# A five-layer transformer kernel: where its two rotary layers make their tables and turn their tiles

## The chip, the cores and the metric

The kernel runs on one core of a Trainium2 chip. The metric is the device time of one execution in microseconds (us). The core has five engines: TensorE (PE), VectorE (DVE), ScalarE (ACT), GpSimd (POOL) and SyncE (SP), each with an instruction queue of its own. They are synchronized by semaphores that the kernel sets by hand.

## What is computed

Five layers over 512 tokens of width 1024, in float32: a first hybrid layer, and then layers 0 to 3 with four different mixers (mLSTM, sliding-window attention, HGRN2, differential attention), each with a feed-forward network (FFN) behind it. Two of them use rotary positions, layers 1 and 3. Cut to what matters here:

```python
def partial_rope(x, positions):           # first 16 of 64 channels of a head
    ang = positions[..., None] * inv      # inv: 8 frequencies
    cos, sin = jnp.cos(ang), jnp.sin(ang)
    x1, x2 = x[..., :8], x[..., 8:16]
    return concatenate([x1 * cos - x2 * sin, x2 * cos + x1 * sin, x[..., 16:]])

def swa_mixer(h, positions, w_in, sinks, w_out):      # layer 1
    proj = h @ w_in                                   # q: 1024, k: 128, v: 128 columns
    q, k = partial_rope(q), partial_rope(k)           # then attention in a window of 128, with sinks

def diff_mixer(h, positions, lam_init, w_in, lam_vec, norm_w, w_out):   # layer 3
    proj = h @ w_in                                   # q, k, v: 1024 columns each
    q, k = partial_rope(q), partial_rope(k)
    lam = exp(sum(lv[0] * lv[1])) - exp(sum(lv[2] * lv[3])) + lam_init
    a = softmax(q0 k0) - lam * softmax(q1 k1)         # causal, per head
```

## The kernel before

Activations lie transposed, 128 channels on the partitions by 512 tokens. Weights come in **slots** of 128 x 1024 (eight 128 x 128 chunks). SyncE loads a slot into `raw`, ScalarE rounds it into `w_hi` (L1202), GpSimd subtracts to get `w_lo` (`low`, L562), and TensorE takes three products per chunk (high by high, low by high, high by low, `slot_products`, L659 to L661). Four slots rotate (`RING`), so ScalarE's split of slot k + 4 waits until TensorE has used slot k. A tile of 128 output channels is one slot; it goes to one of four PSUM banks in turn, and the tile four later waits until VectorE has copied the bank out (`lin_free`).

A layer goes: input projection, mixer, output projection, layer norm, FFN up (44 slots), FFN down (8 tiles of 3 slots), layer norm. The next layer's input projection starts with three tiles (`EARLY`) that are multiplied chunk by chunk as the norm delivers them (L747 to L752). While the FFN runs, VectorE also computes the next layer's modulation from the `ada` weights (L2131) in `ada_raw` and `ada_acc`; TensorE sums it up behind the first down tile, and VectorE stores it in `mod` (L2137, L2170). Then `add_gated` copies the down tiles and keeps sums beside them (L1703 to L1739). ScalarE's part of that is `squares_beside`.

The order on every engine is the order of the code. There is no scheduler; whatever stands behind a waiting instruction on its engine waits too.

In the two rotary layers before the change:

- GpSimd fetches the positions (L625) at the start of the layer. VectorE makes the angles (`rope_tables`, L1936 to L1949: a conversion, ten operations with one source, six with two) right after its copy of tile 3 (`rope_between`), and ScalarE takes their sine and cosine (L1380) into `rope_cs`.
- VectorE's `keep` copies the tiles of the projection to `proj` (L1672). A tile is rotated by `turned_halves` on TensorE (L979: a product with a constant matrix that swaps the two halves, to bank 4 or 5) and three operations of `rope` on VectorE (L1957 to L1959).
- Layer 1 has 9 tiles (8 of queries, then the keys) and one value tile that is multiplied in four quarters (L716 to L718). TensorE turns two tiles behind each quarter, and the ninth at the end. Then VectorE copies the values (L1679), and the rotated keys to `swa_k` (L2204), and attention starts with a score product (L863).
- Layer 3 has 16 tiles (8 of queries, 8 of keys) and 8 value slots that give two groups of four value banks (L703 to L705, copied at L1685). Two tiles are turned behind each value slot. Then GpSimd makes each key tile's two padded copies (`df_k`, L631 and L634), VectorE and ScalarE compute lambda (`lambdas`), and attention starts (L863).

Of the kernel before, what the change touches and what calls it, by code (L numbers as in the profile page):

```python
# [8 lines left out]
F32 = mybir.dt.float32  # L9
# [7 lines left out]
P = 128  # L17
S = 512
# [35 lines left out]
SWA_TILES = [j * P for j in range(9)]  # L54
# [3 lines left out]
DIFF_TILES = [j * P for j in range(16)]  # L58
# [4 lines left out]
           2: (HGRN_TILES, HGRN_VALUES), 3: (DIFF_TILES, DIFF_VALUES)}  # L63
GATE_TILES = {0: [2048 + j * P for j in range(8)], 2: [3072 + j * P for j in range(8)]}
# [42 lines left out]
KEPT = {"ident": 128, "ones": 128, "block64": 128, "eps6": 1, "tiny": 1, "eps6_32": 1, "eps5": 1}  # L107
# [4 lines left out]
def constants():  # L112
# [35 lines left out]
    for at in (2, 4):  # L148
        layer[at, :, 0:128] = rope
        layer[at, :, 128:129] = inv  # L150
# [5 lines left out]
    return kept, big, layer  # L156
# [6 lines left out]
def mix_steps(part):  # L163

    return {"first": 2, 1: 1, 3: 1}.get(part, 0)
# [49 lines left out]
def program(nc, xT, wstream, ada, cols, kept, bigc, layerc, pos, yT, parts):  # L215
    slots_total = stream_length(parts)
    ctx = ExitStack()
    with ctx:
# [96 lines left out]

        ident, ones, block64 = kept_at("ident"), kept_at("ones"), kept_at("block64")
# [242 lines left out]
        def _(pool):  # L559
# [57 lines left out]
            for at, part in enumerate(parts):  # L617
# [18 lines left out]
                if part == 1:  # L636
                    low_to(first_slot + LEAD + 2)
                    nc.gpsimd.memset(swa_k[:, :, :, :], 0.0)
# [10 lines left out]
        def _(pe):  # L649
# [326 lines left out]
            def turned_halves(t):  # L976

                wait(pe, sm.rope_out, n["rope"] - 1)
                mm(bank[4 + n["rope"] % 2][:, :], lc[:, 0:128], proj[:, t, :], start=True,  # L979
                   stop=True).then_inc(sm.rope_mm, 1)  # L980
                n.add(rope=1)

# [141 lines left out]
            for at, part in enumerate(parts):  # L1124
# [14 lines left out]
                linear(len(tiles) - EARLY, h_hi, h_lo, [8])  # L1139
                if part == "first":  # L1140
                    first_values()
                elif part in (1, 3):
                    pe.wait_ge(sm.layer_const_loaded, 16 * n["lc"])
                    if part == 3:
                        pe.wait_ge(sm.lin_free, n["mt"])
# [1195 lines left out]
```

## Time and profile before

| | us |
|---|---|
| median of three runs (range) | 3570.35 (3568.2 to 3574.76) |
| the profiled execution | 3571.12 |
| its span on the core | 3569.1 |
| TensorE busy, share of the span | 3373.3, 95% |
| VectorE busy | 1700.5, 48% |
| ScalarE busy | 1218.1, 34% |
| GpSimd busy | 1314.2, 37% |
| mean granted clock of TensorE | 0.964 |

The page gives busy time per engine, the span in 40 slices and the costliest groups of instructions. The timeline lists instructions in order of time; in brackets stands how long the engine had been idle before one, and what released it. Matmuls are pipelined, and the duration of one in a row is longer than the distance to the next.

### The profile page before, as it was taken

How to read it: one execution, taken by the hardware profiler on the slowest of the kernel's cores; microseconds unless marked ns; L12 is line 12 of the kernel's file. 1: busy time of each engine (PE TensorE's matmuls, PEld its weight loads, DVE VectorE, ACT ScalarE, POOL GpSimd, SP SyncE). 2: the span in 40 equal slices, each digit the busy share in tenths (PEclk: the TensorE clock that was granted, in tenths of full speed). 3: DMA queues.
4: the chain of work that ended last, by engine and by line, in shares of the span. 5: the costliest groups of instructions: out<-in, count | busy, mean ns of one | idle time of the engine just before them, and what ended most of it. 6: DMA issues, size and time to landing. Idle time of an engine off the chain costs nothing.

```text
span 3569.1 us, 43233 instructions
## 1 busy us (share of the span) xinstructions
PE 3373.3 (95%) x15372; PEld 2673.9 (75%) x15372; DVE 1700.5 (48%) x2643; ACT 1218.1 (34%) x1906; POOL 1314.2 (37%) x603
## 2 busy tenths in 40 slices
PE   7987899999989999989999999999999998999998
PEld 6765578886757888767788878767888775668886
DVE  2344545512246554377655343556654347662223
ACT  3246433222234332336432243124332332643322
POOL 3430134443313444430444444433444443024442
PEclk9978999999999999989999999999999998999999
DMA  4310045532212554320455423102554331013332
GB/s 136 106 36 1 24 154 184 186 130 88 77 36 96 198 184 157 103 60 8 147 188 182 142 90 99 44 29 82 202 187 159 109 90 52 1 48 112 94 101 70
DMA packets 102534, 374.08 MB, mean 105 GB/s; under 512 B 11392, under 2 KB 11520, under 8 KB 102272
## 3 DMA queue, kind: packets, MB, share of 16 engines
q1 hardware_dynamic: 102240, 371.77, 31.8%
q8 instruction: 85, 1.39, 0.2%
q0 software_dynamic: 160, 0.52, 0.0%
q14 instruction: 49, 0.40, 0.0%
HBM read 370.15 MB, written 2.10 MB: 104 GB/s over the span
## 4 chain that ended last, share of the span: by engine, by line
issue 44%; PE 41%; POOL 13%; DVE 1%; ACT 1%; DMA 0%; POOLq 0%; SPq 0%; DVEq 0%; ACTq 0%
POOL w_lo L562 12%; PE bank L659 11%; PE bank L661 11%; PE bank L660 11%; PE bank L1092 1%; PE bank L703 1%; PE bank L704 1%; PE bank L705 1%; PE bank L1108 1%; PE bank L1061 0%; PE bank L1001 0%; PE bank L999 0%; PE bank L1000 0%; PE bank L908 0%; PE bank L1134 0%
## 5 line engine op out<-in xcount | busy, mean ns | idle before, releaser
L562 POOL TENSOR_TENSOR w_lo<-raw,w_hi 128x1024 fp32r<-128x1024 f32 x501 | 1226.9, 2455 | 2147.2 <-ACT w_hi L1202 2147.1
L1202 ACT ACTIVATE w_hi<-raw 128x1024 fp32r<-128x1024 f32 x501 | 525.9, 1057 | 1268.9 <-PE bank L661 1054.2
L659 PE MATMUL bank<-h_hi,w_hi 128*128 128x512 f32 x2264 | 888.5, 392 | 15.0 <-POOL w_lo L562 8.2
L661 PE MATMUL bank<-h_hi,w_lo 128*128 128x512 f32 x2264 | 883.1, 390 | 0.0
L660 PE MATMUL bank<-h_lo,w_hi 128*128 128x512 f32 x2264 | 883.1, 390 | 0.0
L659 PEld LDWEIGHTS bank<-h_hi,w_hi 128*128 128x128 f32 x2264 | 426.4, 188 | 109.0 <-POOL w_lo L562 10.7
L661 PEld LDWEIGHTS bank<-h_hi,w_lo 128*128 128x128 f32 x2264 | 426.2, 188 | 89.4
L660 PEld LDWEIGHTS bank<-h_lo,w_hi 128*128 128x128 f32 x2264 | 426.3, 188 | 88.8 <-issue 1.0
L2131 DVE SCALAR_TENSOR_TENSOR ada_acc<-ada_raw,cond,ada_acc 128x1024 f32<-128x1024 f32 x168 | 271.8, 1618 | 236.4 <-DMA ada_raw<-ada 235.2
L659 PE MATMUL bank<-hid_hi,w_hi 128*128 128x512 f32 x880 | 344.4, 391 | 0.0
L661 PE MATMUL bank<-hid_hi,w_lo 128*128 128x512 f32 x880 | 342.5, 389 | 0.0
L660 PE MATMUL bank<-hid_lo,w_hi 128*128 128x512 f32 x880 | 342.4, 389 | 0.0
L2147 DVE TENSOR_TENSOR hid_lo<-layer_const,hid_hi 128x512 f32 (+1 forms) x110 | 221.7, 2015 | 108.4 <-ACT hid_hi L1476 108.4
L660 PEld LDWEIGHTS bank<-hid_lo,w_hi 128*128 128x128 f32 x880 | 165.2, 188 | 35.0 <-issue 1.0
L659 PEld LDWEIGHTS bank<-hid_hi,w_hi 128*128 128x128 f32 x880 | 165.2, 188 | 35.0 <-issue 1.0
L661 PEld LDWEIGHTS bank<-hid_hi,w_lo 128*128 128x128 f32 x880 | 165.2, 188 | 34.6
L1711 DVE SCALAR_TENSOR_TENSOR x<-bank,mod,x 128x512 f32<-128x512 f32 x64 | 48.0, 750 | 286.2 <-PE bank L661 276.0
L2144 DVE TENSOR_TENSOR layer_const<-bank,layer_const 128x512 f32<-128x512 f32 x110 | 75.8, 689 | 209.2 <-PE bank L661 178.6
L1471 ACT ACTIVATE layer_const<-bank 128x512 f32<-128x512 f32 x110 | 65.5, 595 | 313.2 <-PE bank L661 304.1
L747 PE MATMUL bank<-h_hi,w_hi 128*128 128x512 f32 x360 | 154.4, 429 | 17.6 <-ACT h_hi L1274 9.8
L748 PE MATMUL bank<-h_hi,w_lo 128*128 128x512 f32 x360 | 149.5, 415 | 0.0
L1672 DVE COPY proj<-bank 128x512 f32<-128x512 f32 x68 | 45.5, 688 | 213.3 <-PE bank L661 203.8
(345 smaller groups left out, 4235.0 us busy)
## 6 DMA issues: line engine op xcount, KB each, us to landing
raw<-weights SPq DMA_DIRECT2D x501, 512.0 KB, 3.6
ada_raw<-ada SPq DMA_DIRECT2D x192, 512.0 KB, 4.4
layer_const<-layer_const SPq DMA_DIRECT2D x5, 512.0 KB, 4.6
x<-x_t SPq DMA_DIRECT2D x1, 2048.0 KB, 8.1
y_t<-x SPq DMA_DIRECT2D x8, 256.0 KB, 2.0
tables<-big_const SPq DMA_DIRECT2D x1, 768.0 KB, 8.9
cols<-columns SPq DMA_DIRECT2D x1, 573.5 KB, 9.1
rope_i<-positions POOLq DMA_DIRECT2D x2, 256.0 KB, 4.5
```

The costliest lines, as they stand in the source:

```text
L562: nc.gpsimd.tensor_tensor(w_lo[k % RING][:, :, :], raw[k % RING][:, :, :], w_hi[k % RING][:, :, :].bitcast(F32), ALU.subtract).then_inc(sm ...
L659: mm(out, w_hi[r][:, at, :], hi, start=first and at == 0, stop=False)
L660: mm(out, w_hi[r][:, at, :], lo, start=False, stop=False)
L661: op = mm(out, w_lo[r][:, at, :], hi, start=False, stop=last and at == len(pairs) - 1)
L747: mm(out, w_hi[r][:, c, :], h_hi[:, c, :], start=c == 0, stop=False)
L748: mm(out, w_lo[r][:, c, :], h_hi[:, c, :], start=False, stop=False)
L1202: fn(w_hi[t % RING][:, :, :], raw[t % RING][:, :, :], ACT.Copy).then_inc(sm.hi_done, 1)
L1471: fn(sil[q % 2], bank[(mt + 2 * q) % 4][:, :], ACT.Silu).then_inc(sm.sil_done, 1)
L1711: op = v.scalar_tensor_tensor(x[:, m, :], b[:, :], mod_col(layer, sub, ONE_GATE, m), x[:, m, :], ALU.mult, ALU.add)
L2131: op = v.scalar_tensor_tensor(ada_acc[:, :], ada_raw[a % ADA_RING][:, :], cond[:, kc:kc + 1], ada_acc[:, :], ALU.mult, ALU.add)
L2144: v.tensor_tensor(sil[q % 2], bank[(mt + 2 * q + 1) % 4][:, :], sil[q % 2], ALU.mult).then_inc(sm.lin_free, 2)
L2147: v.tensor_tensor(hid_lo[:, q + 4 * i, :], sil[q % 2], hid_hi[:, q + 4 * i, :].bitcast(F32), ALU.subtract).then_inc(sm.part_lo, 1)
```

## The change

The tables are no longer made in the rotary layer but in the down projection of the FFN ahead of it. Their buffers move to the `ada` area and to the input's area `h_at`, the frequencies move from the layer's constants to the kept ones. VectorE makes them between the modulation and `add_gated`, ScalarE takes the sines after its ninth split of the down projection, and GpSimd fetches the positions once the last up tile is copied. In the projection the key tiles come first; TensorE turns tiles 0 and 1 behind tile 3 and tile t - 2 behind each later tile t (`rotated_beside`), VectorE rotates them there, and the last two are turned behind the first two value slots or quarters. The copies to `swa_k`, the padded keys and lambda move beside the projection as well.

```diff
-SWA_TILES = [j * P for j in range(9)]
+SWA_TILES = [j * P for j in (8, 0, 1, 2, 3, 4, 5, 6, 7)]
-DIFF_TILES = [j * P for j in range(16)]
+DIFF_TILES = [j * P for j in (*range(8, 16), *range(8))]
+PLACES = {1: [8, *range(8)], 3: [*range(8, 16), *range(8)]}
+ROTARY = (1, 3)
+def rotated_beside(t):
+    return [] if t < 3 else [0, 1] if t == 3 else [t - 2]
...
-        rope_cs = place("rope_cs", [P, 2, S], F32, big + 12288)
-        rope_t = [place(f"rope_t{r}", [P, S], F32, big + 13312 + r * S) for r in range(4)]
-        rope_i = place("rope_i", [P, S], I32, big + 13312 + 4 * S)
+        rope_cs = place("rope_cs", [P, 2, S], F32, ada_at)
+        rope_t = [place(f"rope_t{r}", [P, S], F32, ada_at + (2 + r) * S) for r in range(4)]
+        rope_i = place("rope_i", [P, S], I32, h_at)
... GpSimd
-                if part in (1, 3):
-                    low_to(first_slot + LEAD)
-                    pool.wait_ge(sm.lin_free, lin_total(parts[:at]))
+                if part in ROTARY:
+                    low_to(first_slot - 3 * DT + LEAD)
+                    pool.wait_ge(sm.lin_free, lin_total(parts[:at]) - DT)
                     pool.dma_start(rope_i[:, :], pos).then_inc(sm.pos_loaded, 16)
                 if part == 3:
-                    low_to(first_slot + len(tiles) + len(values) + LEAD)
                     for hd in range(8):
-                        pool.wait_ge(sm.rope_out, len(SWA_TILES) + 8 + hd + 1)
+                        low_to(first_slot + LEAD + 4 + hd)
+                        pool.wait_ge(sm.rope_out, len(SWA_TILES) + hd + 1)
... TensorE
+            def turned_halves(part, r):
+                pe.wait_ge(sm.lin_free, lin_total(parts[:parts.index(part)]) + r + 1)
                 wait(pe, sm.rope_out, n["rope"] - 1)
+            def rotated_linear(part, tiles, hi, lo, chunks):
+                pe.wait_ge(sm.layer_const_loaded, 16 * n["lc"])
+                for t in range(EARLY, tiles):
+                    m_tile(n["slot"], n["mt"], 0, 0, 0, hi, lo, chunks)
+                    n.add(slot=len(chunks), mt=1)
+                    for r in rotated_beside(t):
+                        turned_halves(part, r)
...
-                    if part == 3:
-                        pe.wait_ge(sm.lin_free, n["mt"])
-                        for t in range(2 * s, min(2 * s + 2, len(tiles))):
-                            turned_halves(t)
+                    def last_turned(s):
+                        if s < 2:
+                            turned_halves(part, last + s)
... ScalarE
+                    if m == 2 and rotary:
+                        rope_tables()
-                elif part in (1, 3):
-                    split_ahead(8)
-                    rope_tables()
+                elif part == 3:
+                    split_ahead(12)
+                    act.wait_ge(sm.lam_in, 1)
+                    fn(lam_w[:, 2:4], lam_w[:, 0:2], ACT.Exp).then_inc(sm.lam_exp, 1)
... VectorE
+                    v.tensor_copy(proj[:, places[t], :], tile_done(1)[:, :]).then_inc(sm.lin_free, 1)
                     between(t)
+                    if part in ROTARY:
+                        rope([places[r] for r in rotated_beside(t)])
+                if part in ROTARY:
+                    rope(places[-2:])
-                    rope(range(tiles))
-                        if rotated and t % TT == 0:
-                            rope(range(2 * t, 2 * t + 8))
...
+            def swa_keys(t):
+                if t == 5:
+                    dve.wait_ge(sm.swa_zero, 1)
+                    dve.wait_ge(sm.rope_out, 1)
...
+            def lambdas(t):
+                if t == 8:
...
+                elif t == 15:
+                    dve.wait_ge(sm.lam_exp, 1)
...
                     ffn(ahead, layer)
+                    if ahead in ROTARY:
+                        rope_tables()
                     add_gated(3, layer, 1, sums_down, None if ahead is None else (ahead, 0), 2 * part + 1)
```

How instructions move on the engines that wait for each other, at three places (line numbers of each program). VectorE in the input projection of layer 1, before: the copy of tile 3 (the last of the first row's four) is followed by all of the tables (`rope_t`, of which the first two operations stand here).

```order
L1672 COPY proj<-bank 128x512 x4
L1964 TENSOR_SCALAR small<-cols 128x16
L1936 CAST rope_t_132<-rope_i 128x512
L1937 TENSOR_SCALAR rope_t_131<-rope_t_132,layer_const 128x512
L1941 TENSOR_SCALAR rope_t_132<-rope_t_131 128x512
```

The same place in the change: two rotations stand behind that copy, and one behind each later one.

```order
L1692 COPY proj<-bank 128x512 x4
L1979 TENSOR_TENSOR rope_t_130<-bank,rope_cs 128x512
L1980 TENSOR_TENSOR proj<-proj,rope_cs 128x512
L1981 TENSOR_TENSOR proj<-proj,rope_t_130 128x512
L1979 TENSOR_TENSOR rope_t_129<-bank,rope_cs 128x512
L1980 TENSOR_TENSOR proj<-proj,rope_cs 128x512
L1981 TENSOR_TENSOR proj<-proj,rope_t_129 128x512
L1692 COPY proj<-bank 128x512
```

The copies of the projection no longer stand behind the tables. VectorE in the down projection of layer 0, before: behind the modulation's two operations (`mod`) comes `add_gated`.

```order
L2137 TENSOR_TENSOR mod_74<-bank,cols 128x8
L2170 TENSOR_SCALAR mod_74<-mod_74 128x2x16
L1618 TENSOR_TENSOR ln_cols<-cols,mod_74 128x8
L1619 TENSOR_TENSOR ln_cols<-cols,mod_74 128x8
L1620 TENSOR_TENSOR ln_cols<-ln_cols,mod_74 128x8
```

In the change the 18 instructions of the tables stand between them, here the first three,

```order
L2164 TENSOR_TENSOR mod_74<-bank,cols 128x8
L2197 TENSOR_SCALAR mod_74<-mod_74 128x2x16
L1956 TENSOR_SCALAR small<-cols 128x16
L1958 CAST rope_t_132<-rope_i 128x512
L1959 TENSOR_SCALAR rope_t_131<-rope_t_132,kept 128x512
```

and here the last three, ahead of the first operations of `add_gated`:

```order
L1968 SCALAR_TENSOR_TENSOR rope_t_130<-rope_t_132,rope_t_130 128x512
L1970 TENSOR_SCALAR rope_t_130<-rope_t_130 128x512
L1971 TENSOR_SCALAR rope_t_130<-rope_t_130 128x512
L1637 TENSOR_TENSOR ln_cols<-cols,mod_74 128x8
L1638 TENSOR_TENSOR ln_cols<-cols,mod_74 128x8
```

Everything of `add_gated`, the copies of the down tiles among it, now stands behind the tables. GpSimd at the end of the input projection of layer 3, before: the pairs of padded keys follow each other behind the last split's loop.

```order
L562 TENSOR_TENSOR w_lo_62<-raw_54,w_hi_58 128x1024
L195 REGISTER_ALU
L195 COMPARE_AND_BRANCH
L631 TENSOR_SCALAR df_k<-proj,kept 128x512
L634 TENSOR_SCALAR proj<-proj,kept 128x512
```

In the change a split of one slot stands between two pairs:

```order
L643 TENSOR_SCALAR proj<-proj,kept 128x512
L571 TENSOR_TENSOR w_lo_63<-raw_55,w_hi_59 128x1024
L640 TENSOR_SCALAR df_k<-proj,kept 128x512
L643 TENSOR_SCALAR proj<-proj,kept 128x512
L571 TENSOR_TENSOR w_lo_64<-raw_56,w_hi_60 128x1024
L640 TENSOR_SCALAR df_k<-proj,kept 128x512
```

So a pair now waits for its key tile's rotation in the middle of the projection, with the later splits behind it in the queue.

## Rows read from the trace of the kernel before

**Rows 1.** The page: busy time and share; the group of GpSimd's splits.

```profile
PE 3373.3 (95%) x15372; PEld 2673.9 (75%) x15372; DVE 1700.5 (48%) x2643; ACT 1218.1 (34%) x1906; POOL 1314.2 (37%) x603
...
L562 POOL TENSOR_TENSOR w_lo<-raw,w_hi 128x1024 fp32r<-128x1024 f32 x501 | 1226.9, 2455 | 2147.2 <-ACT w_hi L1202 2147.1
```

**Rows 2.** Timeline of TensorE, layer 1: start us, us, operation, [idle before].

```profile
1525.00 0.39 PE L659 MATMUL bank<-h_hi,w_hi 128*128 128x512 f32 x1
...
1558.56 0.79 PE L659 MATMUL bank<-h_hi,w_hi 128*128 128x512 f32 x1 [5.90 <-DVE proj L1672]
...
1565.75 0.22 PE L716 MATMUL bank<-w_hi,h_hi 128*128 128x128 f32 x1
...
1568.38 1.93 PE L979 MATMUL bank<-proj,layer_const 128*128 128x512 f32 x4
...
1572.78 1.93 PE L979 MATMUL bank<-proj,layer_const 128*128 128x512 f32 x4
...
1593.98 2.50 PE L863 MATMUL bank<-swa_k,proj 128*128 128x128 f32 x6 [5.27 <-DVE swa_k L2204]
```

**Rows 3.** Timeline of VectorE in the projection of layer 1: the tables.

```profile
1531.25 5.15 DVE L1964 TENSOR_SCALAR small<-cols 128x16 f32<-128x16 f32 x1
...
1536.70 2.50 DVE L1937 TENSOR_SCALAR rope_t<-rope_t,layer_const 128x512 f32<-128x512 f32 x1
...
1551.45 0.41 DVE L1941 TENSOR_SCALAR rope_t<-rope_t 128x512 f32<-128x512 f32 x1
...
1554.27 2.71 DVE L1946 SCALAR_TENSOR_TENSOR rope_t<-rope_t,rope_t 128x512 f32<-128x512 f32 x1
...
1557.82 2.48 DVE L1672 COPY proj<-bank 128x512 f32<-128x512 f32 x4
```

**Rows 4.** Timeline of TensorE, layer 3.

```profile
2866.74 0.39 PE L659 MATMUL bank<-h_hi,w_hi 128*128 128x512 f32 x1
...
2974.96 0.77 PE L703 MATMUL bank<-w_hi,h_hi 128*128 128x512 f32 x1 [5.74 <-DVE df_v L1685]
...
3016.93 0.76 PE L863 MATMUL bank<-proj 128*128 128x128 f32 x2 [11.26 <-POOL proj L634]
```

**Rows 5.** Timeline of VectorE, layer 1: one of its nine rotations, the stretched one.

```profile
1582.68 0.69 DVE L1957 TENSOR_TENSOR rope_t<-bank,rope_cs 128x512 f32<-128x512 f32 x1 [0.46 <-PE bank L979]
1583.29 2.57 DVE L1958 TENSOR_TENSOR proj<-proj,rope_cs 128x512 f32<-128x512 f32 x1
```

**Rows 6.** Timeline of ScalarE, down projection of layer 0: ninth and tenth split.

```profile
1423.53 1.06 ACT L1202 ACTIVATE w_hi<-raw 128x1024 fp32r<-128x1024 f32 x1 [3.02 <-PE bank L661]
1428.97 1.06 ACT L1202 ACTIVATE w_hi<-raw 128x1024 fp32r<-128x1024 f32 x1 [4.38 <-PE bank L661]
```

**Rows 7.** Timeline of VectorE: the last value copies of layers 1 and 3.

```profile
1590.68 1.28 DVE L1679 COPY swa_v<-bank 128x512 f32<-128x512 f32 x2
...
3011.33 2.47 DVE L1685 COPY df_v<-bank 128x512 f32<-128x512 f32 x4
```

**Rows 8.** Timeline of VectorE, down projection of layer 0: modulation, first and fourth tile.

```profile
1393.59 1.75 DVE L2170 TENSOR_SCALAR mod<-mod 128x32 f32<-128x32 f32 x1
...
1399.85 0.75 DVE L1711 SCALAR_TENSOR_TENSOR x<-bank,mod,x 128x512 f32<-128x512 f32 x1
...
1438.50 0.75 DVE L1711 SCALAR_TENSOR_TENSOR x<-bank,mod,x 128x512 f32<-128x512 f32 x1 [13.55 <-PE bank L661]
```

**Rows 9.** Timeline of GpSimd, start of layer 3's attention: one of sixteen paddings.

```profile
3015.65 0.69 POOL L634 TENSOR_SCALAR proj<-proj,kept 128x512 f32<-128x512 f32 x1
```

**Rows 10.** The page, DMA issues: KB each, us from issue to landing.

```profile
rope_i<-positions POOLq DMA_DIRECT2D x2, 256.0 KB, 4.5
```

**Rows 11.** Busy us by stretch, then PEclk, DMA: mLSTM's start, layer 3's attention start.

```profile
956.00:960.00 4.00, 4.00 (x6) 1.77 (x6) 0.00 (x0) 0.00 (x0) 0.00 (x0) 0.50 0.45 131
...
3017.00:3021.00 4.00, 3.92 (x12) 2.60 (x13) 2.40 (x11) 1.72 (x8) 3.51 (x6) 0.50 0.00 0
```

**Rows 12.** Timeline of TensorE: the first product of the mLSTM mixer.

```profile
954.63 2.04 PE L1028 MATMUL bank<-ml_rows,layer_const 4*128 4x512 f32 x2 [2.62 <-issue]
```

More of the change, by code:

```diff
@@ L155, in constants @@
     layer[4, :, 256:768] = causal
-    return kept, big, layer
+    return np.concatenate([kept, inv], 1), big, layer
 PARTS_SPLIT = 3 * DT + FT
 def mix_steps(part):
-    return {"first": 2, 1: 1, 3: 1}.get(part, 0)
+    return {"first": 2, 1: 1}.get(part, 0)
 def n_groups(part):
@@ L1138, in _ @@
                     mlstm_gates()
-                linear(len(tiles) - EARLY, h_hi, h_lo, [8])
+                if part in ROTARY:
+                    rotated_linear(part, len(tiles), h_hi, h_lo, [8])
+                else:
+                    linear(len(tiles) - EARLY, h_hi, h_lo, [8])
                 if part == "first":
@@ L1142, in _ @@
                 elif part in (1, 3):
-                    pe.wait_ge(sm.layer_const_loaded, 16 * n["lc"])
-                    if part == 3:
-                        pe.wait_ge(sm.lin_free, n["mt"])
-                    def two_tiles(s):
-                        if part == 1 and s == 0:
-                            pe.wait_ge(sm.lin_free, n["mt"] - 1)
-                        for t in range(2 * s, min(2 * s + 2, len(tiles))):
-                            turned_halves(t)
-                    value_tiles(len(values), two_tiles)
-                    if part == 1:
-                        two_tiles(TT)
+                    last = len(tiles) - 2
+                    def last_turned(s):
+                        if s < 2:
+                            turned_halves(part, last + s)
+                    value_tiles(len(values), last_turned)
                 else:
@@ L1247, in ln_col, with squares_beside @@
                 return ln_cols[:, kind, c:c + 1]
-            def squares_beside(slots):
+            def squares_beside(slots, rotary=False):
                 done = 0
@@ L1557, in _ @@
                     ffn()
-                    squares_beside(3)
+                    squares_beside(3, at + 1 < len(parts) and parts[at + 1] in ROTARY)
                     if at + 1 < len(parts):
@@ L1667, in tile_done, with keep @@
                 return bank[(n["mt"] - 1) % 4]
-            def keep(tiles, values, between=lambda t: None, rotated=False):
+            def keep(part, tiles, values, between=lambda t: None):
+                places = PLACES.get(part, range(tiles))
                 for t in range(tiles):
-                    v.tensor_copy(proj[:, t, :], tile_done(1)[:, :]).then_inc(sm.lin_free, 1)
+                    v.tensor_copy(proj[:, places[t], :], tile_done(1)[:, :]).then_inc(sm.lin_free, 1)
                     between(t)
+                    if part in ROTARY:
+                        rope([places[r] for r in rotated_beside(t)])
+                if part in ROTARY:
+                    rope(places[-2:])
                 if len(values) == 1:
-                    rope(range(tiles))
                     dve.wait_ge(sm.swa_zero, 1)
@@ L2185, in _ @@
                                     ALU.add).then_inc(sm.gate_pre, 1)
-                    keep(len(tiles), [], first_between)
+                    keep(part, len(tiles), [], first_between)
                     first_values()
@@ L2191, in _ @@
                     vals = {0: ml_v, 1: swa_v, 2: hg_v, 3: df_v}[part]
-                    keep(len(tiles), [swa_v] if part == 1 else
+                    keep(part, len(tiles), [swa_v] if part == 1 else
                          [vals[:, t, g * S:(g + 1) * S] for g in range(D // S) for t in range(TT)],
-                         {0: mlstm_gates, 1: rope_between, 2: hgrn_gates, 3: rope_between}.get(part, lambda t: None), part == 3)
+                         {0: mlstm_gates, 1: swa_keys, 2: hgrn_gates, 3: lambdas}[part])
                 dve.wait_ge(sm.layer_const_loaded, 16 * n["lc"])
@@ L2200, in _ @@
                 elif part == 1:
-                    dve.wait_ge(sm.rope_out, n["rope"])
-                    for g in range(2):
-                        for e, b in enumerate((0, HD)):
-                            op = v.tensor_copy(swa_k[b:b + HD, e, g, :], proj[HD * g:HD * g + HD, 8, :])
-                    op.then_inc(sm.mix_ready, 1)
                     attention(swa_jobs(), AT["late"])
```

46 lines of the change are left out of this document (20 added, 26 removed).

## The prediction

> **What bounds the kernel now.** I read the page first: TensorE is busy for 95% of the span [rows 1], so time can only be won where it stands still or runs at half clock. The chain that ended last goes down GpSimd's weight splits and says nothing of the layers in question, so I went on to TensorE's timeline in the two rotary layers, and from each gap to the engine that ended it. In the sliding-window layer the row to see is the second [rows 2]: TensorE stands for 5.90 us in the middle of the projection until VectorE copies a bank out. VectorE was not copying because it made the rotary tables from 1531.25 to 1557.8 [rows 3]. Then, after the value tile, TensorE turns the last tiles and waits for their rotation, and the first score product starts at 1593.98. In the differential layer it turns two tiles behind each value slot, waits 5.74 us for VectorE between the two value groups, and 11.26 us for GpSimd's padded keys ahead of the first score at 3016.93 [rows 4].
>
> **The projections, part by part.** I rebuild TensorE's road from the first matmul of tile 3 to the first score, with prices from rows.
>
> A weight slot of 24 matmuls takes 5.44 us: ScalarE's splits follow TensorE slot by slot, 1423.53 to 1428.97 [rows 6]. A quarter of the single value tile takes 2.63 us (1565.75 to 1568.38), and a quarter with a pair of turns 4.40 us (1568.38 to 1572.78) [rows 2]; a pair is thus 1.77 us. The trace has no single turn between two tiles. Half a pair, 0.88, is the lower bound; the whole pair, 1.77, the upper one. I take 0.90, since nearly all of a pair is its own streaming. No turn is added or removed (9 and 16), each is only put elsewhere.
>
> Sliding-window layer: 1525.00 + 6 slots of 5.44 (32.6) + 9 turns (8.1) + 4 quarters (10.6) = 1576.3. Behind it comes the copy of the values, 1.28 us [rows 7], with about 0.4 us for the two semaphores. The key copies have gone to tile 5, beside a matmul tile, and cost nothing there. First score at 1578.0 instead of 1593.98: **16.0 us gained**.
>
> Differential layer: 2866.74 + 13 slots (70.7) + 8 value slots (43.5) + 16 turns (14.4) + some 0.85 us for the first copy between the value groups = 2996.2. The last four copies take 2.47 us [rows 7], with 0.4 us for semaphores 2.9. First score at 2999.1 instead of 3016.93: **17.8 us gained**. The GpSimd padding (0.69 us each, two per key tile [rows 9]) now stands behind the splits of single slots. With a split of 2.4 us [rows 1] that is 3.8 us in a period of 6.3; what is queued behind it, the next slot's split, is used by TensorE four slots later. The lambda steps are five small operations on VectorE in tiles 8 and 15, which wait for nothing that comes late; their exponential stands behind ScalarE's twelfth split, when its input is long there.
>
> For this VectorE has to keep pace. Per tile it now does the copy (0.69) and three operations of a rotation (0.69 each where nothing stretches one), 2.8 us; the rotation's second operation took 2.57 us where GpSimd ran beside it [rows 5]. If its second and third both took that every time, 6.6 us would stand against a period of 6.34. The lower bound is no cost; the upper one 0.3 us in 19 tiles, 5 us. I take none, since in that rotation one operation was stretched, not two. TensorE's turn of tile t-2 behind tile t waits for a copy that is a period old, so this wait is free as well.
>
> Here the Trainium skill speaks against the change. The row: a table operation with one source took 2.50 us at 1536.70 and 0.41 at 1551.45, the first beside a GpSimd split [rows 3]. GPSIMD Engine Reference (Key points) says that GpSimd shares its memory interfaces with VectorE and that they contend where VectorE uses two ports or has two SBUF inputs. By that rule rotation and tables are open to it wherever they are put, and GpSimd splits a slot in every one; the sum by the row's short values has no cost, by the rule the 5 us above, and what the next part bounds.
>
> **The tables in the down projection ahead.** VectorE is free for them after the modulation step, 1393.59 + 1.75 = 1395.3 [rows 8]. The positions' DMA is issued when the last up tile is copied, before TensorE ends its first down tile, and lands 4.5 us later [rows 10], ahead of that step. The only thing behind it on GpSimd's queue is a split whose input isn't there yet. The chain took 26.6 us before [rows 3], so it ends near 1422. Behind it wait VectorE's column and sum steps, 4.5 us, and the copy of the first down tile, 1.5 us: 1428 instead of 1401. TensorE wants that bank for its fifth down tile, when the fourth is done: 1438.5 [rows 8]. **10 us of slack, nothing lost.** ScalarE takes its two sines behind its ninth split, at 1424.6, and its next is due at 1428.97 [rows 6]; 1.3 us fit. If VectorE's cover were gone, each us beyond 37 us of tables would be one on TensorE, twice. Lower bound nothing; upper bound, ten one-source operations at 2.50 us, six with two sources at 2.71 and the first two (sinks, conversion to float) at 5.15 [rows 3], is 52 us of tables; I take nothing, since the measured chain already ran beside splits.
>
> **The clock.** TensorE ran at half clock (1.2 GHz) in the first microseconds of the differential attention: 0.50 [rows 11]. I let that stand. In the mLSTM layer the wait before the mixer is 2.62 us [rows 12], about what it will be here, and the granted clock is 0.50 behind it too [rows 11]. So no gain; if the clock stayed at 2.4 GHz, two stretches of some 7 us at half clock would shrink by half, 7 us together.
>
> **Sum.** 16.0 + 17.8 = 33.8 us off the profiled execution's 3571.12: **3537 us**. Its time is 0.8 us above the median of the three runs, well inside their 6.6 us.
>
> **Rivals.**
> 1. The clock holds through the shorter gaps at the attentions' start. For it: the gaps get shorter, in layer 3 from 11.26 us to under 3. Against: the row at 956. It gives 3537.3 - 7 = 3530. Chance 8%.
> 2. VectorE is stretched by GpSimd in the projections and TensorE falls a little behind in each tile, or single turns cost more than half a pair (21 of them, up to 0.87 each). It gives 3537 + 5 to 18, that is 3542 to 3555. Chance 9%.
> 3. The other side: the tables make the down projection late. The decisive place is the bank of the first down tile. Beyond 37 us of tables TensorE stands at tile five and ScalarE's splits stand behind the sines as well. With 52 us that is 15 us, and after such a pause half clock for some 8 us, 4 us more; twice 19 = 38 us, more than the gain: 3575. It decides from a chain of about 50 us. Against it: 26.6 us measured beside the same splits, which are no denser there (one per slot). Chance 2%; a lesser lateness, 3 to 15 us in all, 3%.
> 4. The change does not do what it says: another wait keeps the attention's start (the last rotation, a semaphore behind a copy), and one of the layers wins nothing, the other all. It gives 3571 - 17 = 3554. Against it: each input of the first score is ready at least 3 us before the last value product by the sums above. Chance 3%.
>
> **Numbers.** The forecast keeps 75%, with 3537. The range 3528 to 3549 takes in the clock's 7 us below, and above the 5 us of the stretched rotations, small lateness and part of the single turns' bound; what lies outside is under 2 in 10. About 0.2% (7 us) is what a measurement of this kernel can tell from no change. Faster by more: all but rival 3's worst and accidents that take 27 us back, 0.95. Same 0.03, slower 0.02.
>
> **What would show it.** TensorE: no wait on a bank copy in the window layer's projection, a single turn behind each tile of about 0.9 us, first score some 53 us behind the first matmul of tile 3 there (69 before) and 132 us in the differential layer (150 before). VectorE: tables right behind the modulation step in the down projections of layers 0 and 2, ended under 37 us later. Wrong would be: TensorE idle in the fifth down tile, a period well over 6.4 us between VectorE's copies, or a first score that still waits for GpSimd.

## The result and the profile after

The change makes the kernel faster: 3539.68 us median (3534.65 to 3542.75, four runs) against 3572.56 us (3568.2 to 3575.2, four runs on the same chip). The ratio is 0.9906, with a 95% interval of 0.9894 to 0.9918. That is 32.9 us by the medians; the prediction's sum was 33.8. Four times of either kernel range over 7 and 8 us, so that the two lie this close is in part luck; the windows below are the better test. The profiled execution after took 3542.75 us, with a span of 3541.0.

TensorE's timeline in layer 1 (start us, us, operation, [idle before]), which answers to [rows 2]: first product of tile 3, the pair of turns behind it, two of the single turns, the turn behind the value tile's first quarter, the first score.

```profile
1527.49 0.39 PE L669 MATMUL bank<-h_hi,w_hi 128*128 128x512 f32 x1
...
1532.94 1.88 PE L990 MATMUL bank<-proj,layer_const 128*128 128x512 f32 x4
...
1546.47 1.02 PE L990 MATMUL bank<-proj,layer_const 128*128 128x512 f32 x2
...
1552.80 1.02 PE L990 MATMUL bank<-proj,layer_const 128*128 128x512 f32 x2
...
1568.94 1.07 PE L990 MATMUL bank<-proj,layer_const 128*128 128x512 f32 x2
...
1580.36 0.68 PE L873 MATMUL bank<-swa_k,proj 128*128 128x128 f32 x4 [1.50 <-issue]
```

The wait of 5.90 us is gone. A tile with a single turn takes 6.33 us (1546.47 to 1552.80), of which a slot is 5.44 us, so that a single turn costs 0.89 us. The first score stands 52.87 us behind the first product of tile 3; it was 68.98. The last pause is 1.50 us, about what VectorE's copy of the values takes (1.29 us in a row further down).

The same in layer 3, for [rows 4]:

```profile
2854.20 0.39 PE L669 MATMUL bank<-h_hi,w_hi 128*128 128x512 f32 x1
...
2949.30 1.02 PE L990 MATMUL bank<-proj,layer_const 128*128 128x512 f32 x2
...
2962.10 0.47 PE L713 MATMUL bank<-w_hi,h_hi 128*128 128x512 f32 x1 [0.88 <-DVE df_v L1706]
...
2986.73 0.46 PE L873 MATMUL bank<-proj 128*128 128x128 f32 x2 [2.62 <-issue]
```

The last turn begins at 2949.30, behind the second of eight value slots. Of the waits of 5.74 and 11.26 us there are 0.88 and 2.62 left. First score 132.53 us behind tile 3's first product, before 150.19.

VectorE's timeline in the down projection of layer 0, for [rows 3, 8]: modulation step, conversion, the only two stretched operations of the tables, their end, and the first and third down tile.

```profile
1396.06 1.75 DVE L2197 TENSOR_SCALAR mod<-mod 128x32 f32<-128x32 f32 x1
...
1397.93 0.42 DVE L1958 CAST rope_t<-rope_i 128x512 f32<-128x512 int32 x1
...
1402.81 2.62 DVE L1963 TENSOR_SCALAR rope_t<-rope_t 128x512 f32<-128x512 f32 x1
...
1408.56 2.51 DVE L1970 TENSOR_SCALAR rope_t<-rope_t 128x512 f32<-128x512 f32 x1
1411.11 0.43 DVE L1971 TENSOR_SCALAR rope_t<-rope_t 128x512 f32<-128x512 f32 x1
...
1418.13 0.75 DVE L1732 SCALAR_TENSOR_TENSOR x<-bank,mod,x 128x512 f32<-128x512 f32 x1
...
1426.02 0.75 DVE L1732 SCALAR_TENSOR_TENSOR x<-bank,mod,x 128x512 f32<-128x512 f32 x1 [5.04 <-PE bank L671]
```

The tables take 13.7 us (1397.84 to 1411.54) where they took 26.6 in layer 1. In layer 3 the same instructions took 21.8 us before (2872.99 to 2894.76), and now take 13.7 as well. At the third down tile VectorE already waits for TensorE again, 5.04 us. ScalarE's timeline there, for [rows 6], shows the ninth split, the two sines and the tenth split, which still waits 3.34 us for TensorE:

```profile
1426.01 1.06 ACT L1220 ACTIVATE w_hi<-raw 128x1024 fp32r<-128x1024 f32 x1 [3.02 <-PE bank L671]
1426.98 1.14 ACT L1400 ACTIVATE rope_cs<-rope_t 128x512 f32<-128x512 f32 x2
1431.45 1.06 ACT L1220 ACTIVATE w_hi<-raw 128x1024 fp32r<-128x1024 f32 x1 [3.34 <-PE bank L671]
```

**Where the span went.** Before, the span was 3569.1, after 3541.0, 28.1 us less. The two windows of the layers give 16.11 + 17.66 = 33.8. The rest went the other way: 2.49 us ahead of layer 1's tile 3 (1527.49 against 1525.00), 1.1 us from layer 1's first score to layer 3's tile 3, 2.1 us behind layer 3's first score. None of it arises in the down projections that now hold the tables. At each place where time is lost the profile after has a longer stretch at 1.2 GHz: at the layer norm ahead of layer 3 10.2 us against 6.8, at the end of layer 3's attention 3.4 against none, at the norm behind it 10.2 against 6.8, and near 410 us, in code that the change doesn't touch, where the 2.49 us arise (busy us by stretch of 8 us for TensorE, its weight loads, VectorE, ScalarE, GpSimd, then the granted clock; after, then before):

```profile
404.00:412.00 8.00, 8.00 (x15) 3.91 (x14) 5.77 (x6) 1.34 (x3) 0.00 (x0) 0.50 0.00 0
412.00:420.00 8.00, 8.00 (x25) 4.84 (x24) 2.74 (x5) 1.26 (x2) 0.00 (x0) 0.86 0.00 0
```

```profile
404.00:412.00 8.00, 7.75 (x21) 4.66 (x22) 7.23 (x8) 2.52 (x4) 0.00 (x0) 0.79 0.00 0
412.00:420.00 8.00, 8.00 (x27) 4.16 (x25) 2.69 (x4) 1.26 (x2) 0.00 (x0) 1.00 0.00 0
```

So one profiled pair can be off by some 5 us, and the distance from tile 3's first product to the first score (the **window**) is the better measure below. In the six later runs that keep the change's single turns in full fp32 it is 52.87 us each time, and in layer 3 it stays between 132.32 and 132.69 us in five of them; the sixth moves the padding there.

### The profile page after: what moved, and what is told of

It reads as the page before. It is cut to its first block, busy times and chain, and to the rows that moved or that the text cites. A ratio compares the mean times of both kernels' runs of the same rounds, so it can differ in the third digit from the quotient of the medians.

```text
span 3541.0 us, 43242 instructions
## 1 busy us (share of the span) xinstructions
PE 3371.7 (95%) x15372; PEld 2673.1 (75%) x15372; DVE 1712.6 (48%) x2642; ACT 1215.5 (34%) x1904; POOL 1317.6 (37%) x603
## 4 chain that ended last, share of the span: by engine, by line
PE 43%; issue 42%; POOL 13%; DVE 1%; ACT 1%; DMA 0%; POOLq 0%; SPq 0%; DVEq 0%; ACTq 0%
POOL w_lo L571 12%; PE bank L669 11%; PE bank L671 11%; PE bank L670 11%; PE bank L1112 1%; PE bank L713 1%; PE bank L715 1%; PE bank L714 1%; PE bank L1128 1%; PE bank L1081 0%; PE bank L757 0%; PE bank L758 0%; PE bank L762 0%; PE bank L1021 0%; PE bank L1019 0%
```

## The experiments

My theory: the change is the sum of two parts that don't touch each other, and the slack of the down projection hides the first. The rivals: later waits take the gain back; the tables, or the place of the keys, carry most of it; the clock does.

**The tables alone.** The kernel before, with the tables in the down projection, everything else as it was.

```diff
                     ffn(ahead, layer)
+                    if ahead in (1, 3):
+                        rope_tables()
                     add_gated(3, layer, 1, sums_down, None if ahead is None else (ahead, 0), 2 * part + 1)
...
-                elif part in (1, 3):
-                    split_ahead(8)
-                    rope_tables()
-                    split_ahead(len(tiles) + len(values) - 8)
```

> The kernel before, with the tables alone made in the down projection ahead; tiles are turned and rotated behind the value slots as before. Theory 1 (the two halves of the change add up independently): only the 5.90 us that TensorE waits in layer 1's projection goes, since in layer 3 the copies caught up by themselves; everything behind it (turns, rotations, GpSimd's padding, 5.27 and 11.26 us before the first scores) stays. 3571 - 6 = 3565, that is 0.17% faster than before. Theory 2 (the tables were the real cost and the place of the turns is worth little): most of the 33 us come with this part alone, 3545. Theory 3 (later waits take the 5.90 us back): 3571, no gain.

Measured: 3561.14 us, ratio 0.9976 (0.9965 to 0.9987), 8.6 us by the medians. TensorE's first score in both layers:

```profile
1587.19 1.19 PE L864 MATMUL bank<-swa_k,proj 128*128 128x128 f32 x4 [5.62 <-DVE swa_k L2201]
...
3004.85 0.77 PE L864 MATMUL bank<-proj 128*128 128x128 f32 x2 [11.24 <-POOL proj L634]
```

Both waits ahead of the scores stand as before (5.27 and 11.26 there), so theory 1 holds. In layer 1 the window shrinks from 68.98 to 60.62 us, 8.4 us for a wait of 5.90: behind that wait TensorE had also run at 1.2 GHz for 3.5 us, here not. That is 1.7 us of the other 2.5; the rest is spread in small pieces over the window. The stretches of the kernel before, then of this one:

```profile
1555.00:1559.00 4.00, 0.44 (x1) 0.44 (x2) 3.93 (x5) 1.31 (x3) 1.44 (x1) 0.52 0.33 82
1559.00:1563.00 4.00, 4.00 (x12) 3.12 (x12) 1.30 (x3) 0.00 (x0) 0.00 (x0) 0.62 0.14 53
```

```profile
1555.00:1559.00 4.00, 4.00 (x19) 3.34 (x18) 0.00 (x0) 0.11 (x1) 2.39 (x1) 1.00 0.20 45
1559.00:1563.00 4.00, 4.00 (x29) 3.44 (x29) 0.69 (x1) 1.06 (x1) 2.32 (x1) 1.00 0.32 117
```

The other part, turning and rotating beside the projection, needs the early tables and was not run alone. As the difference it is worth 60.62 - 52.87 = 7.8 us in layer 1 and 149.52 - 132.53 = 17.0 us in layer 3.

**The padded keys late.** In the changed kernel GpSimd pads behind all splits again.

```diff
                 if part == 3:
+                    low_to(first_slot + len(tiles) + len(values) + LEAD)
                     for hd in range(8):
-                        low_to(first_slot + LEAD + 4 + hd)
```

> The changed kernel with GpSimd's padded keys put back behind all splits of layer 3's projection. Theory 1: the padding of the first head begins when the fourth split ahead is done, some 3.6 us after the last value slot (1.06 us ScalarE, 2.45 us GpSimd), and takes 1.4 us; the first score comes 5 us after the last value product instead of 2.9, so 2 to 3 us are lost: 3542. Theory 2: the half-clock stretch at the start of the attention, 3.4 us in the changed kernel and 13.7 before, grows back with the pause, and each us of it costs half a us: 3 to 5 us more, 3546. Theory 3: the padding itself was what made the 11.26 us of before: 8 us or more, 3548.

Measured: 3543.0 us, ratio 0.9918 (0.9902 to 0.9935). The first score is 134.82 us behind tile 3's first product, 2.3 us more. GpSimd's timeline shows the fourth split ahead and the first head's padding:

```profile
2987.51 2.34 POOL L571 TENSOR_TENSOR w_lo<-raw,w_hi 128x1024 fp32r<-128x1024 f32 x1 [3.04 <-ACT w_hi L1220]
2989.83 0.69 POOL L640 TENSOR_SCALAR df_k<-proj,kept 128x512 f32<-128x512 f32 x1
2990.61 0.69 POOL L643 TENSOR_SCALAR proj<-proj,kept 128x512 f32<-128x512 f32 x1
```

Theory 1 is right on the wait. A further 1.8 us are lost in the first 10 us of the attention, where the granted clock is 0.50 from 2989 to 2999 (10.2 us, against 3.4 in the changed kernel's profile), so theory 2 has a part. But the stretch is no fixed mark of either kernel: in a second profile of the unaltered change (the last run below) it is 6.8 us. The 8 us of theory 3 are out. In the kernel before, GpSimd had padded the first head's keys by 3009.67. VectorE's last rotation ended at 3011.4, its copies of the values at 3013.8 and lambda, with a wait for ScalarE's exponential in it, at 3016.7; its last step (L2212) releases TensorE. VectorE's timeline there:

```profile
3016.18 0.16 DVE L2119 TENSOR_TENSOR small<-small 128x1 f32<-128x1 f32 x1 [1.57 <-ACT small L1531]
...
3016.57 0.15 DVE L2212 COPY small<-kept 128x1 f32<-128x1 f32 x1
```

That road, and not the padding that the row of the wait names, led up to the score at 3016.93.

**The keys last.** The old order of tiles; swa_k copied behind the last rotation, padding eight tiles later.

```diff
-SWA_TILES = [j * P for j in (8, 0, 1, 2, 3, 4, 5, 6, 7)]
+SWA_TILES = [j * P for j in range(9)]
...
-                if t == 5:
+                if t == 9:
...
-                        low_to(first_slot + LEAD + 4 + hd)
+                        low_to(first_slot + LEAD + 12 + hd)
```

> The changed kernel with the tiles in the old order, keys last; swa_k is copied behind the last rotation and the padded keys are made beside the last eight tiles and the first value slots. Theory 1 (the order of tiles is worth nothing by itself; what counts is that turn and rotation stand beside the projection): swa_k's four copies fit between the last rotation, 3.4 us before the value copy, and that copy; the padding ends by the third value slot. 3540 within 3 us. Theory 2 (key tiles first is what keeps their copies off the path): the first score of layer 1 comes 1.7 us later, that of layer 3 some us later, 3543 to 3550.

Measured: 3537.24 us, ratio 0.99 (0.9886 to 0.9914), windows 52.87 and 132.33. Theory 1: the order is worth nothing by itself. VectorE's timeline in layer 1 shows why: the four copies of the keys end before TensorE is done with the values, for which VectorE then waits 1.53 us.

```profile
1572.09 0.69 DVE L1983 TENSOR_TENSOR proj<-proj,rope_t 128x512 f32<-128x512 f32 x1
1572.89 1.73 DVE L1992 COPY swa_k<-proj 64x512 f32<-64x512 f32 x4
1576.15 1.29 DVE L1704 COPY swa_v<-bank 128x512 f32<-128x512 f32 x2 [1.53 <-PE bank L728]
```

**Longer tables.** How much slack has the down projection? The six operations that both tables share are done three or five times, with the same values.

```diff
                     r = rope_t[f]
+                    for _ in range(3):
-                    link(v.tensor_scalar(y[:, :], ang[:, :], 1 / (2 * np.pi), shift, ALU.mult, ALU.add))
+                        link(v.tensor_scalar(y[:, :], ang[:, :], 1 / (2 * np.pi), shift, ALU.mult, ALU.add))
...
```

> The changed kernel with the six repeated operations of each table done three times (same values). The chain of the tables measures 13.7 us in the changed kernel; 24 more operations of 0.43 to 0.73 us are 14 us, with the stretched ones some 21: a chain of about 34 us. Theory 1 (the bank of the first down tile decides, 37 us of slack): no change, 3540 within 3 us. Theory 2 (ScalarE's splits behind the two sines decide, with far less slack, since the sines wait for the chain and the tenth split stands behind them): TensorE waits for a split in the down projection, 5 to 15 us in each of two layers, 3550 to 3570.

> The same with the operations done five times: about 38 us of work, 54 us with the stretched ones. Theory 1 (the first down tile's bank, from 37 us on): TensorE stands some 17 us in the fifth down tile of layers 0 and 2, with 2 to 4 us of half clock each: 3540 + 34 + 6 = 3580, slower than the kernel before. Theory 2 (ScalarE's splits): the wait stands before an earlier tile and is longer, above 3590. Theory 3 (the later stages have spare time that takes lateness up): well under 3570.

Measured: three times, 3554.38 us, ratio 0.9947 (0.993 to 0.9964); five times, 3586.26 us, ratio 1.0044 (1.0028 to 1.0061), slower than the kernel before. The place is the one of theory 1 in both, the fifth down tile's bank; TensorE's timelines:

```profile
1444.12 0.80 PE L669 MATMUL bank<-hid_hi,w_hi 128*128 128x512 f32 x1 [5.62 <-DVE sums_down L1736]
```

```profile
1455.93 0.80 PE L669 MATMUL bank<-hid_hi,w_hi 128*128 128x512 f32 x1 [19.75 <-DVE sums_down L1736]
```

The size isn't. With three times the chain is 36.2 us (1395.47 to 1431.67), under my 37, and TensorE already stands 5.62 us. With five it is 50.6 us, and TensorE stands 19.75. Taken off the chains, the pauses put the knee at 30.6 and 30.9 us. VectorE's timeline with three times, behind the chain's last operation (the first row), shows what I had mis-sized:

```profile
1431.24 0.43 DVE L1972 TENSOR_SCALAR rope_t<-rope_t 128x512 f32<-128x512 f32 x1
...
1433.41 2.90 DVE L1727 TENSOR_TENSOR sums_down<-sums_down,x 128x512 f32<-128x512 f32 x1
1436.24 2.88 DVE L1728 TENSOR_TENSOR sums_down<-sums_down,x 128x512 f32<-128x512 f32 x1
1439.15 0.69 DVE L1727 TENSOR_TENSOR sums_down<-sums_down,x 128x512 f32<-128x512 f32 x1
1439.76 2.86 DVE L1728 TENSOR_TENSOR sums_down<-sums_down,x 128x512 f32<-128x512 f32 x1
1442.65 0.75 DVE L1732 SCALAR_TENSOR_TENSOR x<-bank,mod,x 128x512 f32<-128x512 f32 x1
```

Three of the last four sums ahead of the first copy take 2.9 us each instead of 0.69. GpSimd's timeline beside them:

```profile
1433.36 5.20 POOL L571 TENSOR_TENSOR w_lo<-raw,w_hi 128x1024 fp32r<-128x1024 f32 x2 [6.01 <-ACT w_hi L1220]
1439.73 2.34 POOL L571 TENSOR_TENSOR w_lo<-raw,w_hi 128x1024 fp32r<-128x1024 f32 x1 [1.17 <-ACT w_hi L1220]
```

ScalarE's splits had stood behind the second sine, which had waited for the chain. When the chain ended they came in a row, GpSimd's with them, just when VectorE was to free the bank. Behind the pause TensorE runs at 1.2 GHz for another 5.4 us. From the modulation step to tile 3's first product of layer 1 it is 9.5 us more than in the changed kernel for a pause of 5.62, and 23.7 us more for one of 19.75. Of the 3.9 us beyond the pause, 2.6 arise in those 5.4 us, in both runs. Another 1.1 arise only some 65 us later, at the layer norm, where the granted clock is 0.50 for 10.2 us and not 6.8; such differences also stand between profiles of untouched code.

**The pause ahead of the scores filled.** Products of no use into bank 6, one in layer 1 and three in layer 3.

```diff
                     value_tiles(len(values), last_turned)
+                    for _ in range(FILL[part]):
+                        mm(bank[6][:, :], lc[:, 0:128], proj[:, PLACES[part][0], :], start=True, stop=True)
```

> The changed kernel with products of no use (into a bank nobody reads) in the pause before the first score: one in layer 1 (0.9 us), three in layer 3 (2.7 us). They tell what the half clock at the attentions' start costs: 6.8 us at half clock in layer 1 and 3.4 us in layer 3 in the changed kernel. Theory 1 (attention starts slowly because of the scores' way through VectorE and ScalarE, not because of TensorE's clock): the half-clock stretches may vanish, but the time stays within 2 us. Theory 2 (each us at half clock costs half a us, as my prediction priced it): 5 us gained if both vanish, 3535. Theory 3: the clock falls all the same and nothing changes.

Measured: 3540.46 us, ratio 0.9909 (0.9896 to 0.9922): as the changed kernel. Layer 3's attention start, in the changed kernel and in this one (its first score is at 2981.68):

```profile
2987.00:2991.00 4.00, 3.62 (x13) 2.33 (x12) 2.45 (x14) 2.10 (x9) 0.62 (x1) 0.60 0.41 126
2991.00:2995.00 4.00, 3.91 (x21) 2.35 (x21) 2.79 (x11) 2.47 (x8) 0.00 (x0) 0.97 0.01 5
```

```profile
2983.00:2987.00 4.00, 3.48 (x16) 1.70 (x15) 3.09 (x14) 3.09 (x12) 0.00 (x0) 1.00 0.46 131
2987.00:2991.00 4.00, 3.91 (x25) 2.79 (x25) 3.04 (x11) 2.62 (x9) 0.00 (x0) 1.00 0.03 6
```

The clock stays at 2.4 GHz through layer 3's window and attention start. Against 3.4 us at 1.2 GHz in the changed kernel's profile that is worth 0.8 us: a VectorE operation 11.3 us behind the first score comes 10.5 us behind it. Against the 6.8 us in the second profile of the unaltered change it is 1.7 us, and against the 10.2 us of the run with the late padding 2.6. So a us at 1.2 GHz costs about a quarter of a us there. In layer 1 the stretch halves, from 6.8 to 3.4 us, for 0.35 us. Theory 1: TensorE's clock counts for little at the attention's start. That the scores' way through VectorE and ScalarE is what holds it is argued, not shown.

**Turns in two products.** The turns are now most of what TensorE does in the windows beside the projections themselves, 25 of 0.89 us. In this and the next two kernels a tile is split into a high and a low part, as the weights are, and turned in two fast products. The result need not be the full product's to the last bit; how far it moves, no run here tells.

```diff
-                mm(bank[4 + n["rope"] % 2][:, :], lc[:, 0:128], proj[:, PLACES[part][r], :], start=True,
-                   stop=True).then_inc(sm.rope_mm, 1)
+                mm(bank[4 + k % 2][:, :], swap[:, :], t_hi[k % 3][:, :], start=True, stop=False)
+                mm(bank[4 + k % 2][:, :], swap[:, :], t_lo[k % 3][:, :], start=False, stop=True).then_inc(sm.rope_mm, 1)
... VectorE
+                v.tensor_tensor(t_lo[k % 3][:, :], proj[:, place, :], t_hi[k % 3][:, :].bitcast(F32),
+                                ALU.subtract).then_inc(sm.turn_lo, 1)
```

> The changed kernel with each tile split into a high and a low part (ScalarE and VectorE, beside the projection) and turned in two products like the weights' (0.227 us each) instead of one in full fp32 (0.89 us measured). Theory 1 (TensorE's time for a turn is all on the path, the added 0.6 us of ScalarE and 0.7 us of VectorE per tile are not): 25 turns x 0.44 us = 11 us gained, 3529. Theory 2 (VectorE, with up to 5.5 us of work per tile of 5.9 us where a GpSimd split stretches one of its operations by 2 us, falls behind): less than half of that, 3535 to 3545.

Measured: 3542.61 us, ratio 0.9916 (0.99 to 0.9931), no gain; the windows are 52.84 and 131.08 us. The turn itself does what it should: tiles stand 5.90 us apart instead of 6.33. But TensorE waits 3.2 us in either window that it did not wait before. Its timeline shows where, here in layer 1, and VectorE's the operation behind the second wait:

```profile
1533.49 0.50 PE L994 MATMUL bank<-t_hi,swap 128*128 128x512 f32 x1 [2.00 <-DVE t_lo L2003]
...
1567.56 0.50 PE L994 MATMUL bank<-t_hi,swap 128*128 128x512 f32 x1 [1.19 <-DVE t_lo L2003]
```

```profile
1565.00 2.51 DVE L2003 TENSOR_TENSOR t_lo<-proj,t_hi 128x512 fp32r<-128x512 f32 x1 [0.26 <-ACT t_hi L1412]
```

**The low part from the bank.** Same products; the low part is the bank less the high part, there are four buffers, and ScalarE makes a high part one split earlier.

```diff
-                v.tensor_tensor(t_lo[k % 3][:, :], proj[:, place, :], t_hi[k % 3][:, :].bitcast(F32),
-                                ALU.subtract).then_inc(sm.turn_lo, 1)
+                        v.tensor_tensor(t_lo[k % 4][:, :], b[:, :], t_hi[k % 4][:, :].bitcast(F32),
+                                        ALU.subtract).then_inc(sm.lin_free, 1)
```

> Turns in two products again, but with TensorE's waits of the last run removed: each tile's low part is taken from its PSUM bank (an operation with a PSUM source was 0.69 us in every row, also beside a GpSimd split) and four pairs of part buffers instead of three. In the last run a single turn cost 0.46 us instead of 0.89, but TensorE waited 3.2 us for low parts in layer 1 and 3.2 us in layer 3. Theory 1 (those waits, caused by VectorE operations that stood behind GpSimd splits, ate the gain): waits gone, 25 x 0.43 = 10.8 us gained against the changed kernel, first score 49 us behind the first product of tile 3 in layer 1 (52.9) and 125.6 in layer 3 (132.5); 3529. Theory 2 (VectorE is simply too full with a fourth operation per tile): waits of the same size at the same places, 3537 or more.

Measured: 3530.02 us, ratio 0.9876 (0.9859 to 0.9892). The windows are 49.91 and 129.37 us, 3.0 and 3.2 us less than with the change: theory 1 in kind, but 6.1 us rather than 10.8. Waits of 0.53, 1.15, 0.85 and 1.04 us are left, 3.6 of the missing 4.7 us; the other 1.1 I can't place.

**Fewer waits**, and the changed kernel once more beside it.

```diff
-    return [] if t < 3 else [0, 1] if t == 3 else [t - 2]
+    return {0: [], 1: [], 2: [], 3: [0], 4: [1, 2]}.get(t, [t - 2])
...
+                        if t == tiles - 1:
+                            rope([places[r] for r in rotated_beside(t)])
```

> The last run's kernel with its four waits of TensorE attacked: tile 0 alone is turned behind tile 3 and tiles 1 and 2 behind tile 4 (waits of 0.53 and 1.15 us for a low part, 0.85 us for a rotation), and the low part of the last tile is made ahead of the rotation beside it (1.04 us ahead of layer 3's value slots). Theory 1: the waits go, 3.5 us plus the slow restart behind each: first score 49.3 us behind the first product of tile 3 in layer 1 (49.91) and some 126 us in layer 3 (129.37), 3526. Theory 2: the pair behind tile 4 meets a fuller VectorE and the waits turn up there in the same size: 3530.

> The changed kernel unaltered, on the chip and in the rounds of the last run, so that the two are compared directly: 3540 within 3 us, first scores 52.87 and 132.5 us behind the first product of tile 3 as in its profile (these two distances hardly vary from run to run, the total does).

Measured: 3528.89 us (3527.84 to 3530.02), ratio to the kernel before 0.9879 (0.9864 to 0.9893); the changed kernel 3536.74 us (3529.84 to 3547.15), 0.9905 (0.989 to 0.9921). The windows are 49.67 and 127.66 us against 52.87 and 132.32, that is 7.9 us less in one profile each, and 7.9 us by the medians. The two intervals still overlap a little, so the windows are the firmer of the two. Of the four waits two are left, of 0.26 us in layer 1 and of 1.91 us for a rotation in layer 3:

```profile
2859.98 0.47 PE L994 MATMUL bank<-t_hi,swap 128*128 128x512 f32 x1 [1.91 <-DVE proj L2004]
```

By its windows this version beats both kernels.

## Why the prediction was right, and where its steps were off

- **The two windows.** Forecast 53.0 and 132.4 us from tile 3 to the first score, measured 52.87 and 132.53. Slots of 5.44, a single turn of 0.89 (taken 0.90) and the copy ahead of the score were as priced. The sum of 33.8 us is met by the windows and, within the runs' scatter, by the medians (32.9; 34.9 with the change's second set of times). All slots were priced at 2.4 GHz, so the sum already held what the kernel before lost at 1.2 GHz inside its windows, 1.7 us behind the 5.90 us wait alone.
- **GpSimd's padding and lambda beside the projection** cost nothing in the window. Where I had put the 11.26 us of before down to the padding, the row's own word, it was VectorE's road (last rotations, value copies, lambda); the sum didn't rest on it.
- **VectorE's pace.** I took no cost with a bound of 5 us, because one operation of a rotation was stretched, not two. Of the 25 rotations' second operations 20 are stretched by a split, of the third ones 2 (both behind a stretched second one), and 8 more of the third ones take 1.06 or 1.07 us beside the padding; no tile has TensorE waiting. Right, and closer than it looked: with a fourth operation per tile the waits were there at once.
- **The chain of the tables.** Taken from before as 26.6 us, measured 13.7. The step "the measured chain already ran beside splits" failed: in layer 1 those splits came in a burst, four in a row in 10.19 us, and the chain's first two operations stood 5.4 us under a split and GpSimd's two memsets, while the down projection has one split per slot. GpSimd's work has to be counted in the new place, not carried over with the duration. The other chain of the same trace, 21.8 us in layer 3, already showed that the duration goes with the place.
- **The slack behind it.** "Column and sum steps, 4.5 us, and the copy, 1.5 us" took 8.0 us in the changed kernel and 12.4 with the threefold tables. So the knee is near 31 us, not 37. As the chain was 13.7 us, 17 us of slack remained instead of 10. The two errors pulled opposite ways, and since slack remained under either they didn't touch the time.
- **Rival 3** (slower than before) would have come where it was placed, at the first down tile's bank. It decided earlier than said: a chain of 50.6 us gave 3586 us, where 52 us were to give 3575. The 4 us for half clock behind such a pause measured 2.6.
- **The clock, rival 1.** The granted clock still falls behind the pause, as said. That a hold would give 7 us, 3.5 in each layer, was wrong: in layer 3, where one run made it hold, it is 0.8 to 1.7 us, for stretches of 3.4 and 6.8 us. The failed step was to count every us at half clock as half a us lost; at the attention's start it is about a quarter. In the projection and the down projection, where TensorE is what the work waits for, that count was about right (1.7 us for 3.5 us behind the wait of before, 2.6 for 5.4 behind the long tables).

Open is what placed the stretches at 1.2 GHz in stages that no kernel here changes; they differ from profile to profile. The two profiles of the unaltered change have spans of 3541.0 and 3532.7 us, and stand at 1.2 GHz for 236 and 223 us in all. If each of those us costs between a quarter and a half, that is an estimated 3 to 6 of the 8.3 us between them.

## What to carry to other kernels

Price a move by rebuilding the bottleneck engine's road through the stage, slot by slot, from what it streams; then ask of each helper only whether it keeps the pace, and test that with a doubled load, since slack can be taken back by work that piles up behind the late part. When work moves beside other work, recount the neighbour's operations in the new place. Of two operations that do the same beside GpSimd, the one with a source in PSUM was the punctual one here.

## What the runs showed of the hardware

**VectorE stands still for GpSimd's splits, whole.** GpSimd's and VectorE's timelines in layer 1's projection, after:

```profile
1554.14 2.39 POOL L571 TENSOR_TENSOR w_lo<-raw,w_hi 128x1024 fp32r<-128x1024 f32 x1 [3.93 <-ACT w_hi L1220]
```

```profile
1553.93 0.69 DVE L1979 TENSOR_TENSOR rope_t<-bank,rope_cs 128x512 f32<-128x512 f32 x1
1554.54 2.54 DVE L1980 TENSOR_TENSOR proj<-proj,rope_cs 128x512 f32<-128x512 f32 x1
1557.11 0.69 DVE L1981 TENSOR_TENSOR proj<-proj,rope_t 128x512 f32<-128x512 f32 x1
```

The second operation begins under the split and ends at 1557.08, 0.55 us behind the split's end at 1556.53. In the kernel before nine of the 25 second operations began under a split; all nine took 2.54 to 2.62 us and ended 0.55 us behind it, the other 16 took 0.67 or 0.68. A table operation with one SBUF source ended 0.28 or 0.29 us behind the split. One with a source in PSUM was not stretched: the copies of the gated sums (`x<-bank,mod,x`) began under a split 29 times before and 33 times after, and none took more than 0.75 us. Nor was one that had begun before the split: four two-source operations of the tables before, 0.69 us each. Under GpSimd's memsets, which only write, three two-source operations of the rotations after took 0.68 and 0.69 us, while the conversion of the positions before, with one source, stood until 0.30 us behind the second memset. I had expected a slowdown, not a full stop. The Trainium skill says so, on the page SBUF — State Buffer, section "SBUF: two separate sides": the pair of ports that VectorE and GpSimd share is an exclusive lock for a whole instruction, taken by VectorE only where it has two SBUF inputs or runs in a mode that uses both its ports. This case's traces agree, with the numbers above.

**What that is worth**: with the low part taken from its PSUM bank the two windows went from 52.84 and 131.08 to 49.91 and 129.37 us with as many operations. A fourth buffer and an earlier high part came with it, and weren't tried apart.
